# Query and key norm weights brought to all partitions through memory, and one gate sum moved ahead of a softmax

## What is computed

```
h = _rmsnorm(x, g_mix[l])
proj = h @ w_in[l]
gate_pre, a_in, na_qkv, dil_qkv, swa_q, swa_kv = jnp.split(proj, IN_SPLITS, axis=-1)
y_a = _conformer_conv(a_in, a_conv_w[l], a_conv_b[l], a_ln_g[l], a_ln_b[l])
y_b = _neighbourhood_attn(_rmsnorm(bq, na_qn[l]), _rmsnorm(bk, na_kn[l]), bv, na_rpb[l])
cq = _partial_rope(_rmsnorm(cq, dil_qn[l]), cos, sin)
ck = _partial_rope(_rmsnorm(ck, dil_kn[l]), cos, sin)
y_c = _dilated_attn(cq, ck, cv)
...
gates = jax.nn.sigmoid(gate_pre.reshape(bsz, seq, N_BRANCH, D_MODEL) + gate_b[l])
mixed = jnp.sum(gates * branch, axis=2)
x = x + mixed @ w_out[l]
x = x + _conv_ffn(_rmsnorm(x, g_ffn[l]), w_up[l], ffn_conv_w[l], ffn_conv_b[l], w_down[l])
```

## Time and profile before

| | us |
|---|---|
| median of three runs | 1430.99 (1430.59 to 1431.66) |
| profiled execution, its own time | 1432.33 |
| span of the profiled execution | 1430.5 |
| PE busy in it | 1413.5 (99%) |
| POOL busy | 1181.8 (83%) |
| ACT busy | 871.4 (61%) |
| DVE busy | 705.0 (49%) |

### The profile page before, as it was taken

How to read it: one execution, slowest core, us unless ns; L and a number is a source line. 1 busy time by engine, 2 the same in 40 slices (tenths; PEclk the granted TensorE clock), 3 DMA queues, 4 the chain that set the end, 5 groups by cost and what they waited for, 6 DMA issues and landing times.

```text
span 1430.5 us, 25158 instructions
## 1 busy us (share of the span) xinstructions
PE 1413.5 (99%) x7898; PEld 1212.6 (85%) x7898; DVE 705.0 (49%) x1595; ACT 871.4 (61%) x1466; POOL 1181.8 (83%) x926
## 2 busy tenths in 40 slices
PE   8999999999999999999999999999999999999998
PEld 8877778888888777788888899998899888888887
DVE  3653554555555733556545555670663611544444
ACT  5665656766676655648666676864444544755555
POOL 5876687999979876887999979899676898799985
PEclk9999999999999999999999999999999999999999
DMA  7764455665656754565666566556443465566662
GB/s 252 217 188 141 143 166 156 198 204 187 186 176 201 231 158 133 163 179 159 206 191 191 191 211 193 156 177 204 133 146 122 157 207 179 163 206 185 192 190 93
DMA packets 137728, 255.02 MB, mean 178 GB/s; under 512 B 7920, under 2 KB 96560, under 8 KB 137264
## 3 DMA queue, kind: packets, MB, share of 16 engines
q1 hardware_dynamic: 128368, 244.81, 55.7%
q10 hardware_dynamic: 9280, 9.15, 2.2%
HBM read 252.84 MB, written 1.08 MB: 178 GB/s over the span
## 4 chain that ended last, share of the span: by engine, by line
PE 96%; ACT 1%; issue 1%; DVE 1%; DMA 1%; POOL 0%; PEld 0%; ACTq 0%; PEldq 0%; DVEq 0%; POOLq 0%; SPq 0%
PE psum L1151 21%; PE psum L1152 20%; PE psum L1153 20%; PE psum L1183 17%; PE psum L1185 9%; PE psum L1270 1%; PE psum L1336 1%; PE psum L1289 1%; PE psum L1280 1%; DMA raw<-in_units 1%; PE psum L1258 0%; PE psum L1337 0%; PE psum L1297 0%; PE psum L1659 0%; PE psum L1399 0%
## 5 line engine op out<-in xcount | busy, mean ns | idle before, releaser
L482 POOL TENSOR_TENSOR w_lo<-raw,w_hi 128x512 fp32r<-128x512 f32 x461 | 602.1, 1306 | 232.4 <-ACT w_hi L514 228.7
L514 ACT ACTIVATE w_hi<-raw 128x1024 fp32r<-128x1024 f32 x461 | 487.4, 1059 | 306.4 <-PE psum L1153 197.4
L483 POOL TENSOR_TENSOR w_lo<-raw,w_hi 128x512 fp32r<-128x512 f32 x461 | 607.4, 1318 | 0.0
L1183 PE MATMUL psum<-both,w_hi 128*128 128x512 f32 x1040 | 259.1, 391 | 0.0
L1183 PEld LDWEIGHTS psum<-both,w_hi 128*128 128x128 f32 x1040 | 190.7, 188 | 36.7
L1151 PE MATMUL psum<-w_hi,both 128*128 128x512 f32 (+1 forms) x544 | 212.9, 391 | 4.9 <-DVEq L2041 4.4
L1152 PE MATMUL psum<-w_hi,both 128*128 128x512 f32 (+1 forms) x544 | 206.1, 379 | 0.0
L1153 PE MATMUL psum<-w_lo,both 128*128 128x512 f32 (+1 forms) x544 | 206.0, 379 | 0.0
L1185 PEld LDWEIGHTS psum<-both,w_lo 128*128 128x128 f32 x1040 | 141.9, 190 | 10.2
L1185 PE MATMUL psum<-both,w_lo 128*128 128x256 f32 x1040 | 145.0, 282 | 0.0
L1835 DVE TENSOR_TENSOR psum<-psum,arena 128x256 f32<-128x256 f32 x136 | 58.6, 433 | 173.6 <-ACT arena L552 173.6
(11 more groups left out here) (299 smaller groups left out, 2168.9 us busy)
## 6 DMA issues: line engine op xcount, KB each, us to landing
raw<-in_units SPq DMA_DIRECT2D x453, 512.0 KB, 3.6
arena<-gate_rows ACTq DMA_DIRECT2D x8, 512.0 KB, 7.4
raw<-in_units SPq DMA_DIRECT2D x8, 384.0 KB, 3.0
arena<-in_consts ACTq DMA_DIRECT2D x1, 2320.0 KB, 8.9
arena<-in_bias ACTq DMA_DIRECT2D x2, 1024.0 KB, 5.2
raw<-in_units SPq DMA_DIRECT2D x8, 128.0 KB, 3.0
out<-arena SPq DMA_DIRECT2D x4, 256.0 KB, 2.7
arena<-in_consts SPq DMA_DIRECT2D x1, 768.0 KB, 7.6
```

The costliest lines, as they stand in the source:

```text
L482: pool.tensor_tensor(w_lo[s][:, 0:D // 2], raw[s][:, 0:D // 2], w_hi[s][:, 0:D // 2].bitcast(F32), ALU.subtract)
L483: pool.tensor_tensor(w_lo[s][:, D // 2:D], raw[s][:, D // 2:D], w_hi[s][:, D // 2:D].bitcast(F32), ALU.subtract)\
L514: act.activation(w_hi[s][:, :], raw[s][:, :], ACT.Copy).then_inc(hi_ready, d.inc(hi_ready))
L1183: pe.matmul(bank(4 + k), blocks_of(w_hi[s], c), both[:, 2 * c * T:2 * (c + 1) * T], start=(c == 0), stop=False, skip_group_check=True)
```

## The change

The weights of the query and key norms go the way of the gate bias. In the parameter table their 11 columns (one for each tile of 128 query or key columns) now stand directly ahead of the 32 columns of the gate bias, so one transpose on PE turns all 43. ACT multiplies the query columns by 1/8 beforehand, in place. ACT stores 43 rows instead of 32, waits for the store right there, and issues three broadcast loads into `hsel`, of 3, 4 and 4 tiles. DVE waits for all three ahead of `gained(0)`. PE's six multiplications and ACT's six copies go; only the angles of layer 0 still go through PSUM. Second, in round 2 `gate_sums(2)` stands ahead of `weights(3, 0)`, the first half of the softmax's division; `gate_sums(3)` stays at the end.

```diff
-P1, NP1 = columns([("g_mix", CH), ("g_ffn", CH), ("gate_b", 4 * CH), ("conv_w", 2 * TAPS), ("conv_b", 2),
-                   ("ln_g", 2), ("ln_b", 2), ("qk_g", QKT), ("sink", 4), ("ffn", 8 * FF1)])
+P1, NP1 = columns([("g_mix", CH), ("g_ffn", CH), ("qk_g", QKT), ("gate_b", 4 * CH), ("conv_w", 2 * TAPS), ("conv_b", 2),
+                   ("ln_g", 2), ("ln_b", 2), ("sink", 4), ("ffn", 8 * FF1)])
...
                 norm(load_params1, P1["g_mix"], 2, True, 0 if layer else 1)
+                query_gains = prm[:, P1["qk_g"]:P1["qk_g"] + 12].rearrange("p (a b) -> p a b", b=4)[:, :, 0:2]
+                act.activation(query_gains, query_gains, ACT.Copy, scale=SCALE).then_inc(gains_scaled, d.inc(gains_scaled))
                 act.dma_start(a1("bias", 0, 4 * 2 * T), t["bias1"][layer])\
                     .then_inc(bias_full, d.inc(bias_full))
...
                     act.wait_ge(d.last, d.made(d.last))
-                    act.dma_start(gate_rows1[layer].rearrange("(k x) -> k x", x=P), a1("sc", 0, P)[0:4 * CH]).then_inc(bias_saved, d.inc(bias_saved))
+                    act.dma_start(gate_rows1[layer].rearrange("(k x) -> k x", x=P), a1("sc", 0, P)[0:QKT + 4 * CH]).then_inc(bias_saved, d.inc(bias_saved))
+                    act.wait_ge(bias_saved, d.next(bias_saved))
+                    for at, first, step, n in ((0, 0, 5, 3), (3, 1, 1, 4), (7, 6, 1, 4)):
+                        rows_of_tiles = gate_rows1[layer:layer + 1, 0:QKT * P].rearrange("a (k x) -> a k x", x=P)[:, first:first + step * (n - 1) + 1:step]
+                        act.dma_start(gain_rows(at, n).rearrange("p (k x) -> p k x", x=P), rows_of_tiles.broadcast_to([P, n, P])).then_inc(gains_full, d.inc(gains_full))
...
-                    for k, (first, step, n) in enumerate(((0, 3, 2), (4, 1, 2), (1, 5, 2), (7, 1, 2), (9, 1, 2), (2, 1, 1))):
-                        rows_of_two = ck("hsel", 0, QKT * P).rearrange("p (t h d) -> p t h d", h=2, d=HD)[:, first:first + step * (n - 1) + 1:step]
-                        row = bank(2, k * HD, HD).unsqueeze(1).unsqueeze(1).broadcast_to([P, n, 2, HD])
-                        last = act.activation(rows_of_two, row, ACT.Copy, scale=1.0 if k % 2 else SCALE)
-                    last.then_inc(gain_ready, d.inc(gain_ready))
...
-                pe.transpose(bank(0, 0, P)[0:4 * CH], prm[:, P1["gate_b"]:P1["gate_b"] + 4 * CH], ident)\
+                pe.wait_ge(gains_scaled, d.next(gains_scaled))
+                pe.transpose(bank(0, 0, P)[0:QKT + 4 * CH], prm[:, P1["qk_g"]:P1["qk_g"] + QKT + 4 * CH], ident)\
                     .then_inc(bias_turned, d.inc(bias_turned))
-                for k in range(6):
-                    last = pe.matmul(bank(2, k * HD, HD), prm[:, P1["qk_g"] + 2 * k:P1["qk_g"] + 2 * k + 1].to_broadcast([P, P]), ident[:, 0:HD],
-                                     start=True, stop=True)
-                last.then_inc(gain_out, d.inc(gain_out))
...
-                dve.wait_ge(gain_ready, d.next(gain_ready))
+                dve.wait_ge(gains_full, d.next(gains_full, 3))
+                if layer == 0:
+                    dve.wait_ge(gain_ready, d.next(gain_ready))
...
-                        gate_sums(GATES_SUMMED[p][0])
+                    early, later = GATES_SUMMED[p][:-1], GATES_SUMMED[p][-1:]
+                    for j in early:
+                        gate_sums(j)
...
-                    for k in GATES_SUMMED[p] if p + 1 < len(PIECES) else GATES_SUMMED[p][1:]:
-                        gate_sums(k)
+                    for j in later:
+                        gate_sums(j)
```

More of the change, by code:

```diff
@@ L214, in ck @@
             return arena[0:parts, A1["consts"] + K1[name] + lo:A1["consts"] + K1[name] + lo + n]
-        gate_rows1 = nc.dram_tensor("gate_rows1", (DEPTH, 4 * D), F32, kind="Internal").ap()
+        gate_rows1 = nc.dram_tensor("gate_rows1", (DEPTH, (QKT + 4 * CH) * P), F32, kind="Internal").ap()
         def gate_home(k, half):
@@ L317, in program @@
         bias_turned, bias_saved = signal("bias_turned"), signal("bias_saved", 16)
+        gains_scaled, gains_full = signal("gains_scaled"), signal("gains_full", 16)
         gate_sum, tanh_ready = signal("gate_sum"), signal("tanh_ready")
@@ L627, in save_gate_bias @@
                     act.wait_ge(bias_turned, d.next(bias_turned))
-                    act.activation(a1("sc", 0, P)[0:4 * CH], bank(0, 0, P)[0:4 * CH], ACT.Copy).then_inc(act_own, d.inc(act_own))
+                    act.activation(a1("sc", 0, P)[0:QKT + 4 * CH], bank(0, 0, P)[0:QKT + 4 * CH], ACT.Copy).then_inc(act_own, d.inc(act_own))
                     act.wait_ge(d.last, d.made(d.last))
-                    act.dma_start(gate_rows1[layer].rearrange("(k x) -> k x", x=P), a1("sc", 0, P)[0:4 * CH]).then_inc(bias_saved, d.inc(bias_saved))
+                    act.dma_start(gate_rows1[layer].rearrange("(k x) -> k x", x=P), a1("sc", 0, P)[0:QKT + 4 * CH]).then_inc(bias_saved, d.inc(bias_saved))
[3 more added lines that the diff above has]
+                        act.dma_start(gain_rows(at, n).rearrange("p (k x) -> p k x", x=P), rows_of_tiles.broadcast_to([P, n, P])).then_inc(gains_full, d.inc(gains_full))
                 def load_gate_bias(n):
-                    if n == 0:
-                        act.wait_ge(bias_saved, d.next(bias_saved))
-                    rows_of_n = gate_rows1[layer:layer + 1].rearrange("a (c n x) -> a n c x", n=4, x=P)[:, n].broadcast_to([P, CH, P])
+                    rows_of_n = gate_rows1[layer:layer + 1, QKT * P:].rearrange("a (c n x) -> a n c x", n=4, x=P)[:, n].broadcast_to([P, CH, P])
                     act.dma_start(a1("gates", n * D, D).rearrange("p (c x) -> p c x", x=P), rows_of_n)\
@@ L647, in _, with spread_angles @@
                 act.activation(small[:, 57:58], small[:, 60:61], ACT.Sqrt)
-                def spread_gains():
+                def spread_angles():
+                    act.wait_ge(consts1_full, 16)
                     act.wait_ge(gain_out, d.next(gain_out))
[L652 to L655, removed]
-                    for k, (first, step, n) in enumerate(((0, 3, 2), (4, 1, 2), (1, 5, 2), (7, 1, 2), (9, 1, 2), (2, 1, 1))):
-                        rows_of_two = ck("hsel", 0, QKT * P).rearrange("p (t h d) -> p t h d", h=2, d=HD)[:, first:first + step * (n - 1) + 1:step]
-                        row = bank(2, k * HD, HD).unsqueeze(1).unsqueeze(1).broadcast_to([P, n, 2, HD])
-                        last = act.activation(rows_of_two, row, ACT.Copy, scale=1.0 if k % 2 else SCALE)
-                    last.then_inc(gain_ready, d.inc(gain_ready))
+                    act.activation(ck("hstat", 0, 4 * ROPE), bank(2, 0, 4 * ROPE), ACT.Copy).then_inc(gain_ready, d.inc(gain_ready))
                 def squares(g):
@@ L690, in _ @@
                 save_gate_bias()
-                spread_gains()
+                if layer == 0:
+                    spread_angles()
                 for g in range(3):
@@ L1432, in _ @@
                             for k in range(4):
-                                last = pe.transpose(bank(2, 6 * HD + k * ROPE, ROPE), ck("sin" if k >= 2 else "cos", k % 2 * P, P, ROPE), ident[0:ROPE, 0:ROPE])
+                                last = pe.transpose(bank(2, k * ROPE, ROPE), ck("sin" if k >= 2 else "cos", k % 2 * P, P, ROPE), ident[0:ROPE, 0:ROPE])
                             last.then_inc(gain_out, d.inc(gain_out))
```

## The result

The changed kernel takes 1438.59 us as the median of seven runs (1435.75 to 1439.79), the kernel before 1432.75 in seven runs beside them. The ratio is 1.0042, 95% interval 1.0032 to 1.0053: 6 us slower. The profiled execution of the changed kernel took 1437.25 us with a span of 1435.5, against 1430.5 before, so 5.0 us of the loss can be read in the traces. The forecast was 1429.4 with a range up to 1433.4.

A forecast was written before the change was run, and what follows sets the result against it. PE bounds the kernel, busy 1413.5 of 1430.5 us, so only its waits count. Terms -4.38 (gate sums), -0.10 (multiplications), +2.90 (weights' round trip) make -1.6 on the median 1430.99: 1429.4 us, range 1426.3 to 1433.4.

The forecast's parts named there:

- Moved sum: PE's wait ahead of gate group 4, round 3, goes in both layers: 4.38 us gained.
- Six multiplications: Before group 0 on PE, 1.45 us a layer: removal gains 0 in layer 0 and 0.10 us in layer 1.
- the waits to be seen: Sign at the start of group 0: PE waits about 2 us in layer 0, 1.3 in layer 1, starts unchanged.
- Copies replaced by a round trip: Weights through memory delay DVE's group 0, then ACT's queries, then PE's group 2: stalls 1.51 + 1.39 = 2.9 us.
- The slack of DVE's start: How late group 0's keys on DVE may be before PE stalls at group 2: 3.52 and 3.04 us.
- the time of landing: Store lands 2.2 and 1.4 us after issue; the three loads land 5.4 us after the first load's issue.
- t: Time from the first weight load's issue to the landing of the third: estimated at 5.4 us.
- the prediction's own formula: PE's stalls before group 2 are t - 3.89 and t - 4.01, together 2t - 7.9, never below 0.
- The bounds named for t: Landing of the weight loads: 4.4 us from a unit load below; 7.4 median, 9.3 once, from bias-row broadcasts above.
- Rival 2: Late weights stall PE before group 2 for more than the gates give: 1433.4 to 1437.2 us, chance 0.2.
- point of decision: Late weights outweigh the gains of 4.48 us once the loads take over 6.2 us to land.
- The estimate by the Trainium skill's fit: Weight loads land in 3.7 us, by 2.0 us plus bytes at 436 GB/s; PE would not stall before group 2.

The follow-up runs named there:

- the early version: Changed kernel with the 43 rows stored after the first of four unit copies and loads issued after the second: 1425.77 us, ratio 0.9959 to the kernel before.
- the last experiment: Changed kernel with one broadcast load of the weights instead of three and 48 stored rows instead of 43: 1431.92 us, ratio 0.9998 to the kernel before.
- the single load: Changed kernel with one broadcast load of all 11 weight columns instead of three, columns in order of use: 1432.63 us, ratio 1.0006 to the kernel before.
- the early sigmoid: Layer 0's second gate sigmoid ahead of the unit copy: changed kernel with earlier store, 1425.19 us; kernel before with moved sum, 1425.41 us.

## Why the prediction was wrong

*Moved sum: right, and too small.* The step "So I take all of the wait: 2 x 2.19 = 4.38 us gained" holds; the moved pair stands in the gap of DVE and the waits are gone. The run of the sum alone gave 6.5 us of span, since the half clock behind the wait of layer 0 went with it. The prediction knew that wait and not what followed it. The row with the clock at 0.51 was there to be read in the trace of before; I had looked at PE's waits alone.

*Six multiplications: the size was right, the sign for it was not.* Leaving them out gives 0.1 us a layer, as the distances from the transpose to group 0 show. But the waits to be seen were put at about 2 and 1.3 us, and 0.99 stood in both layers. The start of group 0 in layer 0 stayed where it was partly by luck: the `high` ahead of ACT's sigmoid, which had made it late before, no longer held it, and PE had come 0.7 us later. What covers the six is a chain of PE's own last unit, ACT's sigmoid and DVE.

*Copies replaced by a round trip: the mechanism was right, two of its terms were mis-sized.* The slack of DVE's start (3.52 and 3.04 us) was right: 1.6 us late cost nothing in the early version, and 7.7 us late gave a wait of 3.96. The step that failed is the time of landing, twice: the store's 2.2 and 1.4 us were taken from one trace of before as if fixed ("43 rows instead of 32 change little"), and for the loads "I take a little less, 5.4 us, an estimate". The first load was issued at 42.99 where I had 41.88, 1.1 us later, and in layer 1 by the same amount (2.59 us after the store where I had 1.5). Whether the 11 more rows have a part in that stays open, since 32 rows took up to 3.4 and 2.6 us in other traces. Then the three loads took t = 7.08 and 7.13 us instead of 5.4. Put into the prediction's own formula, 1.1 + 1.7 more for each layer turns its stalls of 1.51 and 1.39 into 4.3 and 4.2; 3.96 and 3.81 were measured. The bounds named for t had 7.2 inside them; the value between them was chosen towards the plain transfers, and the broadcast, which was the nearest kind, was right.

*Missing term.* Stalls of this size brought a slow stretch each, 1.4 and 1.7 us, which none of the steps had; the one of before (1.7 us) went. The prediction's sum with the measured stalls is 1430.99 - 4.48 + 7.77 = 1434.3, above the range by itself, and with 1.4 us more for the clock 1435.7, a ratio of 1.0033, at the lower end of the measured interval. Rival 2 ("the weights come so late that they cost more than the gates give") is what happened, and I had given it 0.2. Its point of decision, t = 6.2, was passed, and both waits are over its 2.2 us.

*The estimate by the Trainium skill's fit* for t (3.7 us) was far off for three broadcasts beside unit loads; the single large one came to 4.2 and 5.4, and to 4.7 and 6.2 in the last experiment.

## What to carry to other kernels

A value that goes out to memory and back costs two landings in a row, and here the loads' landing changed with how they were cut, and varied from trace to trace: place the store as early as its data allow, and let each consumer wait for its own part alone. When a change trades work in a shadow for latency, work out the slack to the first wait of the bounding engine, then ask which of the two terms, slack or latency, has a row behind it. And take no landing time from a single trace: here the same store took from 1.4 to 2.6 us at one place. When a wait of TensorE is priced, read the granted clock of the microseconds behind it too; here a slow stretch added 1.4 to 1.7 us to waits of 2.2 to 4.0 us.

## What the runs showed of the hardware

PE's clock fell to half at 9 of the 11 waits of 2.19 us and more that stand in the traces of the two kernels and of the ten experiments, and behind none of those of 1.8 us and less that came after the first 10 us (the idle end of a kernel aside). In four of the nine, of waits between 3.4 and 4.3 us, it was low 0.5 to 1.4 us before PE went on; in the others it fell up to 1.2 us after. It was low for 3.4 us in six cases and for 6.8 in three. The same wait of 2.19 us was followed by it in layer 0 and not in layer 1 of the kernel before, so one trace cannot say what a given wait will cost. The timed runs of the kernel before show the same in their mean clock: of 24 beside the experiments from the single load to the early sigmoid, the ten at a mean granted clock of 0.997 took 1433.4 to 1433.9 us and the six at 1.000 took 1430.6 to 1431.3.

A store of 43 rows was followed by the dependent issue after 2.6 to 2.9 us in layer 1, one of 48 rows after 1.5 and 1.65 (two runs); stores of 32 rows landed there after 1.4, 1.4, 2.4 and 2.6. With the earlier issue the weights were hardly there earlier: DVE began 9.3 us after the store of 48 rows with three loads, against 9.7 and 9.3 with 43 rows, and 7.7 with one load, against 7.0.
